# Dilated attention in a two-block kernel: from one head at a time to head pairs

## The reference, cut to what matters

```python
DILATED_PATTERNS = ((128, 1), (512, 4), (2048, 16))
def dilated_sliding_attention(q, k, v):
    for window, d in DILATED_PATTERNS:
        half = window // (2 * d)
        o, lse = banded_attention(to_strided(q, d), to_strided(k, d), to_strided(v, d), half)
        ...
    w = jax.nn.softmax(jnp.stack(lses, axis=0), axis=0)
    o = jnp.sum(w[..., None] * jnp.stack(outs, axis=0), axis=0)
...
    att = dilated_sliding_attention(q, k, v).reshape(B, S, D_ATT)
    conv = conformer_conv(...)            # 31 taps, then layernorm and silu
    h = h + jnp.concatenate([att, conv], axis=-1) @ w_out[l]
```

## Time and profile before

| | |
|---|---|
| median of 3 runs | 3522.06 us (3520.27 to 3522.53) |
| profiled execution, first to last instruction (its span) | 3516.4 us |
| busy in it: PE / DVE / ACT / POOL | 3313.4 / 1391.7 / 843.2 / 1029.6 us |
| first score product to first `w_out` product | 289.1 to 622.9 us |

### The profile page before, as it was taken

How to read it: one execution, slowest core, us unless ns; L and a number is a source line. 1 busy time by engine, 2 the same in 40 slices (tenths; PEclk the granted TensorE clock), 3 DMA queues, 4 the chain that set the end, 5 groups by cost and what they waited for, 6 DMA issues and landing times.

```text
span 3516.4 us, 42356 instructions
## 1 busy us (share of the span) xinstructions
PE 3313.4 (94%) x15334; PEld 2649.5 (75%) x15334; DVE 1391.7 (40%) x1742; ACT 843.2 (24%) x1149; POOL 1029.6 (29%) x1017
## 2 busy tenths in 40 slices
PE   7998998899899999999988989999999999999997
PEld 5775766689588888888865668877677888888885
DVE  5586666442533121212567741115534521212124
ACT  3003555310422010101345630015512210101010
POOL 2321222232033333333322223322133333333331
PEclk9998999999999999999999989999999999999998
DMA  3110000213011111111120112210023111111111
GB/s 113 48 36 12 1 0 13 90 48 102 13 42 48 48 48 49 51 49 48 42 96 30 45 51 72 76 48 14 12 89 120 48 48 48 48 48 48 48 49 64
DMA packets 45744, 176.10 MB, mean 50 GB/s; under 512 B 5200, under 2 KB 5840, under 8 KB 44496
## 3 DMA queue, kind: packets, MB, share of 16 engines
q1 hardware_dynamic: 40464, 145.15, 12.7%
q10 hardware_dynamic: 5184, 29.66, 2.2%
HBM read 161.68 MB, written 13.11 MB: 50 GB/s over the span
## 4 chain that ended last, share of the span: by engine, by line
PE 83%; DVE 11%; ACT 3%; issue 2%; DMA 1%; DVEq 0%; POOL 0%; ACTq 0%; SPq 0%; POOLq 0%
PE psum L394 67%; PE psum L494 5%; PE psum L476 4%; PE psum L484 2%; PE psum L384 1%; DVE t L1354 1%; DVE Z L1379 1%; PE psum L604 1%; DVE I L1377 1%; DVE Z L1372 1%; DVE cacc L1090 1%; DVE rstd L1077 1%; PE psum L653 1%; DMA H<-x 1%; ACT P L787 1%
## 5 line engine op out<-in xcount | busy, mean ns | idle before, releaser
L394 PE MATMUL psum<-A_hi,w_hi 128*128 128x512 f32 x2304 | 724.1, 396 | 44.8 <-DVE A_lo L1067 19.7
L394 PE MATMUL psum<-A_lo,w_hi 128*128 128x512 f32 x2304 | 713.0, 391 | 0.0
L394 PE MATMUL psum<-A_hi,w_lo 128*128 128x512 f32 x2304 | 712.6, 391 | 0.0
L309 POOL TENSOR_TENSOR small<-ident 128x1 f32<-128x1 f32 x256 | 60.0, 235 | 1998.8 <-PE psum L394 1917.8
L315 POOL TENSOR_TENSOR w_lo<-raw,w_hi 128x1024 fp32r<-128x1024 f32 x240 | 597.4, 2489 | 20.1
L394 PEld LDWEIGHTS psum<-A_hi,w_hi 128*128 128x128 f32 x2304 | 433.8, 189 | 147.4 <-issue 41.2
L394 PEld LDWEIGHTS psum<-A_lo,w_hi 128*128 128x128 f32 x2304 | 435.1, 189 | 91.4
L394 PEld LDWEIGHTS psum<-A_hi,w_lo 128*128 128x128 f32 x2304 | 434.6, 189 | 91.2
L394 PE MATMUL psum<-B_hi,w_hi 128*128 128x512 f32 x1472 | 455.2, 390 | 10.1 <-DVE B_lo L1358 10.1
L394 PE MATMUL psum<-B_lo,w_hi 128*128 128x512 f32 x1472 | 453.6, 389 | 0.0
L394 PE MATMUL psum<-B_hi,w_lo 128*128 128x512 f32 x1472 | 453.6, 389 | 0.0
(11 more groups left out here) (196 smaller groups left out, 2922.2 us busy)
## 6 DMA issues: line engine op xcount, KB each, us to landing
raw<-weights SPq DMA_DIRECT2D x256, 512.0 KB, 3.5
H<-x SPq DMA_DIRECT2D x4, 1024.0 KB, 10.4
H<-x ACTq DMA_DIRECT2D x1, 4096.0 KB, 12.4
x_spill<-H ACTq DMA_DIRECT2D x1, 4096.0 KB, 11.1
mixed_spill<-t ACTq DMA_DIRECT2D x8, 512.0 KB, 2.6
BE<-rel_bias ACTq DMA_DIRECT2D x8, 512.0 KB, 4.5
t<-mixed_spill ACTq DMA_DIRECT2D x8, 512.0 KB, 4.5
H<-x_spill ACTq DMA_DIRECT2D x2, 2048.0 KB, 7.7
```

The lines of the kernel that those rows point to most:

```text
L309: pool.tensor_tensor(small[:, 12:13], ident[:, 0:1], ident[:, 0:1], ALU.mult)
L394: last = pe.matmul(PJ[s][:, c:c + step], w[:, s, k, :], b[:, k, c:c + step], start=(k == 0 and i == 0), stop=(k == kblocks - 1 and i == 2))
```

## The change

The attention goes through 32 pairs: query tile `t` of head pair `m`, both heads together.

- Scores: the 64 rows of a head are stationary as they lie in `Q` (64 rows, 128 columns), with 64 rows of `K` moving; the heads alternate, in rows 0 to 63 and 64 to 127 of the array. `QZ` and its copies on GpSimd go.
- VectorE's reduction is written with the scale and the sign inside, so the row maximum needs no instruction of its own. One reciprocal serves both heads.
- GpSimd multiplies the probabilities by the inverse sums (2 operations of 128x1024 in place for each pair), and only then they are turned.
- Values: 64 columns of V stationary, 128 columns of `PT` moving, into partitions 64h to 64h+63 of `PX`; the result has channels on partitions. It stays in `PX` for a whole head pair `m`; ScalarE and VectorE split it in halves of 512 queries. `turn_output` goes here (it stays in the second block).
- `P` gets three buffers for each head, `PT` two. The loops are written out, the order is fixed in each engine's code. The first two weight splits of `w_out` come before the attention on GpSimd instead of behind it.

```diff
@@ buffers @@
-        P1 = [at(f"P1_{i}", o_a + i * KIB4, [SEQ]) for i in range(2)]
-        PT1 = [at(f"PT1_{i}", o_a + (2 + i) * KIB4, [TT, P]) for i in range(2)]
-        QZ1 = [at(f"QZ1_{i}", o_a + 32768 + 512 * i, [P]) for i in range(2)]
+        P1 = [[at(f"P1_{h}{i}", (o_b + 49152 + (2 * i + h) * KIB4) if i < 2 else (o_a + 49152 + h * KIB4), [SEQ])
+               for i in range(3)] for h in range(2)]
+        PT1 = [[at(f"PT1_{h}{i}", o_a + 16384 + (2 * i + h) * KIB4, [TT, P]) for i in range(2)] for h in range(2)]
@@ GpSimd @@
-            pool.wait_ge(S["products"], 2 * ROUNDS["w_out"])
-            zero_stages(QZ1)
-            pool.wait_ge(S["roped"], 8)
-            stage_queries(QZ1, Q, Tally(pool, S["staged"]), S["scores"])
-            splits(ROUNDS["w_out"], ROUNDS["xk"])
+            split(ROUNDS["w_out"], 0)
+            split(ROUNDS["w_out"], 1)
+            for p in range(PAIRS):
+                pool.wait_ge(S["inverted"], p + 1)
+                for h in range(2):
+                    probs = P1[h][p % 3]
+                    pool.tensor_scalar(probs[:], probs[:], rsums[p % 3][:, h:h + 1], 1.0,
+                                       ALU.mult, ALU.mult).then_inc(S["probs"], 1)
+            splits(ROUNDS["w_out"] + 1, ROUNDS["xk"])
@@ TensorE @@
+            def pair_scores(p):
+                m, t = p // TT, p % TT
+                if p:
+                    pe.wait_ge(S["masked"], 2 * p)
+                for c in range(0, SEQ, HALF):
+                    for h in range(2):
+                        rows = slice(DH * h, DH * h + DH)
+                        last = pe.matmul(PJ[h][:, c:c + HALF], Q[rows, m, P * t:P * t + P], K[rows, m, c:c + HALF],
+                                         start=True, stop=True)
+                last.then_inc(S["scores"], 1)
+            def pair_turn(p, part):
+                h, n = part // 2, 4 * p + part
+                pe.wait_ge(S["probs"], 2 * p + h + 1)
+                if n >= 2:
+                    pe.wait_ge(S["copied_t"], n - 1)
+                for k in range(4):
+                    key = P * (4 * (part % 2) + k)
+                    last = pe.transpose(PX[:, HALF * (part % 2) + P * k:HALF * (part % 2) + P * k + P],
+                                        P1[h][p % 3][:, key:key + P], ident[:])
+                last.then_inc(S["probs_t"], 1)
+            def pair_values(p, half):
+                m, t = p // TT, p % TT
+                if half == 0:
+                    pe.wait_ge(S["copied_t"], 4 * p + 4)
+                    if m and t % 4 == 0:
+                        pe.wait_ge(S["attended"], 2 * m - 1 + t // 4)
+                for k in range(4 * half, 4 * half + 4):
+                    for h in range(2):
+                        last = pe.matmul(PX[DH * h:DH * h + DH, 1024 + P * t:1024 + P * t + P],
+                                         V[:, k, 2 * DH * m + DH * h:2 * DH * m + DH * h + DH], PT1[h][p % 2][:, k, :],
+                                         start=(k == 0), stop=(k == TT - 1))
+                if half:
+                    last.then_inc(S["pv"], 1)
             pe.wait_ge(S["roped"], 8)
-            attention(K, V, QZ1, P1, PT1, [0] * TT, [TT] * TT,
-                      ("staged", "scores", "masked", "probs", "probs_t", "copied_t", "pv", "attended"))
+            pair_scores(0)
+            for i in range(PAIRS + 2):
+                if i + 1 < PAIRS:
+                    pair_scores(i + 1)
+                for half in range(2):
+                    if 1 <= i <= PAIRS:
+                        pair_turn(i - 1, 2 * half)
+                        pair_turn(i - 1, 2 * half + 1)
+                    if i >= 2:
+                        pair_values(i - 2, half)
...
-            turn_output(S["o_turned"], S["o_lo"])
+            pe.wait_ge(S["attended"], 8)
@@ ScalarE @@
-            with loop(act, 0, 2, {tallies["probs"]: 32, tallies["copied_t"]: 64, tallies["conv_stored"]: 1}) as mm:
-                for sub in range(2):
-                    for st in range(16):
-                        soft_step(2 * mm + sub, st, [TT] * TT, DH ** -0.5, P1, PT1,
-                                  ("masked", "probs_t", "pv", "probs", "copied_t"))
-                store_conv(mm + 2, mm + 3)
+            def pair_exp(p, h):
+                act.wait_ge(S["masked"], 2 * p + h + 1)
+                probs = P1[h][p % 3]
+                act.activation(probs[:], probs[:], ACT.Exp, bias=lowest[h][p % 3], scale=-1.0,
+                               accum_out=sums[p % 3][:, h:h + 1]).then_inc(S["exped"], 1)
+            def pair_copy(p, part):
+                h = part // 2
+                if p >= 2:
+                    act.wait_ge(S["pv"], p - 1)
+                act.wait_ge(S["probs_t"], 4 * p + part + 1)
+                a = 4 * (part % 2)
+                act.activation(PT1[h][p % 2][:, a:a + 4, :].rearrange("p a b -> p (a b)"),
+                               PX[:, P * a:P * a + HALF], ACT.Copy).then_inc(S["copied_t"], 1)
+            def pair_out_hi(m, half):
+                act.wait_ge(S["pv"], TT * m + 4 * half + 4)
+                act.activation(A_hi[:, m, HALF * half:HALF * half + HALF],
+                               PX[:, 1024 + HALF * half:1024 + HALF * half + HALF], ACT.Copy).then_inc(S["o_hi"], 1)
+            pair_exp(0, 0)
+            pair_exp(0, 1)
+            for i in range(PAIRS + 3):
+                if i >= 3 and (i - 3) % 4 == 3:
+                    pair_out_hi((i - 3) // TT, (i - 3) % TT // 4)
+                for h in range(2):
+                    if 1 <= i <= PAIRS:
+                        pair_copy(i - 1, 2 * h)
+                        pair_copy(i - 1, 2 * h + 1)
+                    if i + 1 < PAIRS:
+                        pair_exp(i + 1, h)
+                if i == 15:
+                    store_conv(2, 3)
+            store_conv(3, 4)
...
-            for m in range(4):
-                act.wait_ge(S["o_turned"], m + 1)
-                tallies["o_hi"](act.activation(A_hi[:, m, :], PJ[m % 2], ACT.Copy))
@@ VectorE @@
-            with loop(dve, 0, 2, {chain: 64 + 30, tl["masked"]: 32, tl["attended"]: 32, tl["conv_done"]: 1}) as mm:
-                for sub in range(2):
-                    def between(st, sub=sub):
-                        if 16 * sub + st < TAPS:
-                            tap(mm + 2, 16 * sub + st)
-                    soft_steps(2 * mm + sub, [0] * TT, [TT] * TT, DH ** -0.5, P1,
-                               lambda t, h: MK[:, SEQ - P - P * t:2 * SEQ - P - P * t],
-                               ("scores", "probs_t", "pv", "masked", "attended"), between)
-                dve.wait_ge(S["conv_stored"], mm + 3)
+            def pair_mask(p, h):
+                t = p % TT
+                if p >= 3:
+                    dve.wait_ge(S["probs_t"], 4 * (p - 3) + 2 * h + 2)
+                dve.wait_ge(S["scores"], p + 1)
+                dve.tensor_tensor_reduce(P1[h][p % 3][:], PJ[h], MK[:, SEQ - P - P * t:2 * SEQ - P - P * t],
+                                         -DH ** -0.5, 3e38, ALU.add, ALU.min,
+                                         accum_out=lowest[h][p % 3]).then_inc(S["masked"], 1)
+            def pair_invert(p):
+                dve.wait_ge(S["exped"], 2 * p + 2)
+                dve.reciprocal(rsums[p % 3], sums[p % 3]).then_inc(S["inverted"], 1)
+            def pair_out_lo(m, half):
+                part = slice(HALF * half, HALF * half + HALF)
+                dve.wait_ge(S["o_hi"], 2 * m + half + 1)
+                dve.tensor_tensor(A_lo[:, m, part], PX[:, 1024 + HALF * half:1024 + HALF * half + HALF],
+                                  f32(A_hi[:, m, part]), ALU.subtract).then_inc(S["attended"], 1)
+            pair_mask(0, 0)
+            pair_mask(0, 1)
+            for i in range(PAIRS + 3):
+                if i < PAIRS:
+                    pair_invert(i)
+                if i + 1 < PAIRS:
+                    pair_mask(i + 1, 0)
+                    pair_mask(i + 1, 1)
+                if i >= 3 and (i - 3) % 4 == 3:
+                    pair_out_lo((i - 3) // TT, (i - 3) % TT // 4)
+                for j in (2 * i, 2 * i + 1):
+                    if j == TAPS + 1:
+                        dve.wait_ge(S["conv_stored"], 3)
+                    if j != TAPS and j <= 2 * TAPS:
+                        tap(2 + j // (TAPS + 1), j % (TAPS + 1))
+            dve.wait_ge(S["conv_stored"], 4)
...
-            for m in range(4):
-                dve.wait_ge(S["o_hi"], m + 1)
-                tl["o_lo"](dve.tensor_tensor(A_lo[:, m, :], PJ[m % 2], f32(A_hi[:, m, :]), ALU.subtract))
```

More of the change, by code:

```diff
@@ L76 @@
 NB_ROWS = 10
+PAIRS = 4 * TT
 class Tally:
@@ L155, in build @@
         rot = at("rot", o + 1536, [P])
-        small = at("small", o + 2048, [76])
+        small = at("small", o + 2048, [100])
         mx, nmx, rsum, rinv = (small[:, 2 * i:2 * i + 2] for i in range(4))
         eps = small[:, 8:9]
```

(12 more changed lines are left out.)

## The result

| | before | after |
|---|---|---|
| median of the runs, us | 3521.16 (3518.32 to 3522.53, 4 runs) | 3413.13 (3411.81 to 3413.75, 4 runs) |
| span of the profiled execution, us | 3516.4 | 3412.0 |
| ratio of the runs | | 0.9696 (95%: 0.9683 to 0.9710) |

The change gained 108 us by the medians and 104.4 us by the spans.

A forecast was written before the change was run, and what follows sets the result against it. TensorE was taken to bound the attention: scores 2.15, transposes 1.76, values 1.84 and shape changes 0.80 make 6.55 us a pair instead of 8.66. With start, drain and tail that gave -76.4, 3446 us, range 3420 to 3515.

The forecast's parts named there:

- The bound: Attention: TensorE stays the bound at 6.55 us a pair, with 0.6 us of slack to VectorE.
- Scores and values: TensorE's products in a pair: staggered overlap of two heads, scores 5 slots or 2.15 us, values 17 slots or 1.84.
- both ends that I had drawn: Score time a pair: 3.44 us with no overlap of the heads, 2.15 with overlap in issue order.
- Shape changes: TensorE in a pair: five changes of tile shape at 0.16 us each, 0.80 a pair.
- Length of the stage: Attention: fourth scores near 314.5, then 30 pairs, 7 us of last work and 5 for stumbles; last values at 326.5 + 30P.
- the 1 us charged for the two weight splits: Before the attention: splits moved beside VectorE's last taps delay the first mask by 1 us, bounds 0 and 7.
- 7 us of drain: End of the attention: the last transposes and two value blocks after the 30 pairs take 7 us.
- 5 us of stumbles: Attention: 5 us added to the 30 pairs, between none and the 17.6 us or so of before.
- Tail: Behind the attention: layernorm's first sum 2 us after the last values; the chain behind it 3.7 us shorter without `turn_output`.
- VectorE, too high: VectorE's work in a pair: masks 2.52, two taps 2.92, with the rest 5.95 us.
- the rival with free shape changes: Attention: shape changes cost nothing, TensorE needs 5.75, VectorE's 5.95 us bounds; -94.4, 3428 us; chance 0.12.

The follow-up runs named there:

- few taps: Changed kernel with 58 of the 62 convolution taps that VectorE does in the attention left out: 3412.89 us, ratio 0.9704 to the kernel before.
- half the transposes: Changed kernel with two of the four 128 x 128 transposes in each part left out, products still issued: 3392.40 us, ratio 0.9639 to the kernel before.
- Scores by head: Changed kernel with a pair's score products issued both halves of head 0, then both of head 1: 3412.05 us, ratio 0.9692 to the kernel before.
- values by head: Changed kernel with each block's value products issued four of head 0, then four of head 1: 3447.26 us, ratio 0.9792 to the kernel before.
- division twice: Changed kernel with GpSimd multiplying each probability tile by 1 before its division: 3423.61 us, ratio 0.9728 to the kernel before.

## Why the prediction was right in kind and off in size

**The bound, right.** TensorE stays the bound, VectorE is next, GpSimd is hidden in the masks; few taps and half the transposes show it.

**Scores and values, the step that failed.** It is the number of slots: "With overlap only of different heads, in issue order ... 8 records take 5 slots", and 17 slots for the values. I had staggered the heads by a slot, as if head 0's second record held head 1's next. Head 1's record starts beside head 0's, so it is 4 and 16 slots: 1.72 and 1.75 (by the slots of the trace) instead of 2.15 and 1.84. That made 6.01 of 6.55 us, and 30 x 0.54 = 16.2 us in the end. Scores by head shows that even the written order would not have staggered them. Full overlap was below both ends that I had drawn, 3.44 and 2.15: the lower end should have been half the time.

**Shape changes, right.** 1.92 - 1.72 = 0.20 behind the scores, 1.02 - 0.87 = 0.15 behind each block of transposes and of values: 0.80 a pair, as charged. This is what the Trainium skill ("TensorEngine Tiling (Array Packing)", Key Properties) calls the drain at a change of mode; the trace agrees, with these gaps at each change and none in the kernel before, where the shape stays. The Trainium skill's rule ("TensorE: Matmul & The Clock Gate", Part 3, What overlaps and what doesn't) that weight loads overlap running products only where the row groups differ is contradicted: both value tiles use all rows, and 16 records with a load each go in eight slots. The Trainium skill ("TensorE: Matmul & The Clock Gate", Part 2, Step-by-step: what each phase is for) also says that products themselves stay in program order. In scores and values by head the second head's records run beside earlier ones of the first; by strict order head 1's first score record could start only with head 0's fourth, three slots of 0.43 later, and the block shows none of that.

**Length of the stage.** The fourth scores came at 314.66 (forecast 314.5), from a mask that came 1.0 us late, the 1 us charged for the two weight splits. That is luck: in the second profiled execution of the same kernel the mask came at 297.83, 0.2 us earlier than before the change, and the two executions are already 1.3 us apart at 66 us. In both the splits did stretch a tap to 3.32 us, but behind the taps VectorE had waited 2.11 us for TensorE, and that wait shrank to 0.21. From there to the end of the last values it was 499.05 - 314.66 = 184.4 = 30 x 6.01 + 4.1 us. I had put 7 us of drain and 5 us of stumbles behind the 30 pairs: 3.0 too many, since the last rounds have no scores and no waits, and 5.0 for stumbles that did not come. The steps before were loops with boundaries and now all is written out; that this is the reason was not tried by itself.

**Tail.** The first sum of the layernorm came 1.6 us behind the last values (2 expected). From it to `w_out` it is 521.08 - 500.67 = 20.4 us instead of 622.90 - 597.66 = 25.2: -4.8, with -3.7 expected.

**VectorE, too high without effect.** Masks are 1.15 apart and two taps take 2.60, not 2.52 and 2.92 a pair, because unrolled taps have no wait of 0.18 between them. With the rest VectorE is busy 117.98 of 140 us, 5.1 us a pair instead of 5.95. The division took 1.12 (1.05 taken). Had VectorE been the bound, as in the rival with free shape changes, its price would have been wrong by some 26 us. That GpSimd and the taps exclude each other, which the prediction read from one row, is what division twice shows.

Sum: -76.4 - 16.2 - 5.0 - 3.0 - 1.5 (both ends of the tail) = -102.1, beside -101.8 measured at `w_out`. The last 2.6 us to the spans' 104.4 come in small steps over the remaining 2900 us, and the other 3.6 to the medians' 108.0 come mostly from the profiled execution of before (3518.32) being 2.8 us faster than its median. Neither was followed.

## What to carry to other kernels

Products on half of the rows or half of the columns ran fully two at a time, so the lower bound of such a change is half the time of those products, plus 0.15 to 0.20 us for every change of shape; only the share that is full-shape work (the transposes here) stays. Alternate the halves at every product, since up to three waiting records (one product and the rest of the running one) were looked past and each record more cost a slot. Where a GpSimd operation stands beside a tap on VectorE, add up their times as one queue, less 0.11 to 0.22 us at each hand-over; beside a mask, which reads PSUM, it costs nothing. Before taking shape changes out, look at what the blocks between them hide.

## What the hardware showed that was not expected

- TensorE's look past waiting records of the other half of the columns: three, by rows of 4, 6 and 8 records (0.05, 0.27 and 0.49 us a block); whether it counts records or products is open.
- A GpSimd operation with one input and a tap on VectorE take turns: what begins beside the other ends its own time, less 0.11 to 0.22 us, behind the other's end (taps 1.84 and 1.94 instead of 1.28, GpSimd 2.01 and 1.96 instead of 1.04 and 1.12).
- A gain of 12 us early in the kernel shrank to 7 in a later stage that does the same work. That stage took 180.5 to 181.8 us in eleven traces and 184.6 to 184.9 in three, at a mean granted clock of 0.98 or 0.99 and of 0.94 or 0.95, without order in the time at which it began.
